# Standing half of the input projection between the steps of self-attention in a fused encoder layer

## The reference

```python
h = rmsnorm(x, norm_mix_g)
proj = h @ w_in
q, k, v, z_sg, gate_logits = jnp.split(proj, IN_SPLITS, axis=-1)
...
attn_branch = block_attention(q, k, v) @ w_attn_o
sg_branch = spatial_gating(jax.nn.gelu(z_sg), sg_norm_g, sg_w, sg_b) @ w_sg_o
g_attn, g_sg = jnp.split(jax.nn.sigmoid(gate_logits), N_BRANCHES, axis=-1)
x = x + (g_attn * attn_branch + g_sg * sg_branch) @ w_out
x = x + cross_attention(rmsnorm(x, norm_xa_g), rmsnorm(mem, norm_mem_g), wq_xa, wkv_xa, wo_xa)
x = x + peer_ffn(rmsnorm(x, norm_ffn_g), w_peer_q, peer_k1, peer_k2, expert_down, expert_up)
```

## Time and profile before

| what | us |
|---|---|
| median of 3 executions | 2597.4 (2597.3 to 2603.41) |
| span of the profiled execution | 2596.5 |
| PE busy in it | 2453.0 (94%) |
| DVE busy | 2168.5 (84%) |
| POOL busy | 1369.1 (53%) |
| ACT busy | 1097.1 (42%) |

### The profile page before, as it was taken

The page is one execution under the profiler, slowest core; times in us unless marked ns, Lnnn a source line. Parts: engine busy times, 40 slices in busy tenths (PEclk is TensorE's granted clock), DMA queues, the critical chain, the costliest instruction groups (busy, mean ns, idle before and its releaser), DMA issues.

```text
span 2596.5 us, 38792 instructions
## 1 busy us (share of the span) xinstructions
PE 2453.0 (94%) x13143; PEld 2072.0 (80%) x13143; DVE 2168.5 (84%) x3950; ACT 1097.1 (42%) x1939; POOL 1369.1 (53%) x1054
## 2 busy tenths in 40 slices
PE   7988999899999999999998889999999999999998
PEld 5767888788876778877876667888888888888987
DVE  6355445886679797877899978999999999999999
ACT  4463444343247313443317993333333333343333
POOL 0000000315742464655665547788788877777875
PEclk9999999999999999999999999999999999999999
DMA  6745545447973788877953559999999999999998
GB/s 249 269 136 178 195 146 178 177 186 270 382 272 114 281 313 320 323 280 259 364 177 135 210 227 402 408 412 415 415 412 415 415 413 415 415 415 400 414 415 310
DMA packets 240423, 787.52 MB, mean 303 GB/s; under 512 B 21904, under 2 KB 75328, under 8 KB 219552
## 3 DMA queue, kind: packets, MB, share of 16 engines
q0 software_dynamic: 112288, 408.77, 40.3%
q1 hardware_dynamic: 128000, 377.00, 39.0%
HBM read 728.01 MB, written 57.67 MB: 303 GB/s over the span
## 4 chain that ended last, share of the span: by engine, by line
PE 33%; DVE 28%; issue 17%; ACT 9%; DMA 8%; POOL 4%; DVEq 1%; POOLq 0%; SPq 0%; ACTq 0%
PE lin L245 9%; PE lin L247 9%; PE lin L246 9%; DVE Y L2454 4%; ACT row_ring L1826 4%; DMA w_raw<-in_up,now 2%; DVE low L2431 2%; DVE w_raw L2440 2%; DVE w_lo L222 2%; DVE low L2420 2%; DVE rows L2440 2%; DVE row_ring L138 2%; PE tr L1755 2%; DMA rows<-in_up,now 2%; DVE gl L2464 1%
## 5 line engine op out<-in xcount | busy, mean ns | idle before, releaser
L150 POOL DMA_INDIRECT row_ring<-in_down,IDX x256 | 365.4, 1428 | 314.2 <-DVE dots L138 241.2
L222 DVE TENSOR_TENSOR w_lo<-w_raw,w_hi 128x2048 fp32r<-128x2048 f32 x100 | 230.1, 2301 | 227.5 <-ACT w_hi L214 213.5
L245 PE MATMUL lin<-w_hi,T_hi 128*128 128x512 f32 x976 | 389.2, 399 | 15.6 <-DVE w_lo L222 7.2
L247 PE MATMUL lin<-w_hi,T_lo 128*128 128x512 f32 x976 | 388.4, 398 | 0.0
L246 PE MATMUL lin<-w_lo,T_hi 128*128 128x512 f32 x976 | 385.9, 395 | 0.0
L214 ACT ACTIVATE w_hi<-w_raw 128x2048 fp32r<-128x2048 f32 x116 | 221.8, 1913 | 351.7 <-PE lin L247 334.4
L2313 POOL DMA_INDIRECT rows<-in_up,now x192 | 309.0, 1609 | 64.7 <-issue 53.9
L138 DVE CUSTOM_DVE_ANT_0 row_ring<-row_ring,H 128x1024 f32<-128x1024 f32 x256 | 302.9, 1225 | 33.6 <-DMA row_ring<-in_down,IDX 32.9
L245 PE MATMUL lin<-w_hi,c_hi 128*128 128x512 f32 x768 | 307.1, 400 | 17.5 <-DVE c_lo L2467 17.3
L2313 POOL DMA_INDIRECT w_raw<-in_up,now x189 | 277.6, 1469 | 84.3 <-issue 43.8
L245 PE MATMUL tr<-T_hi,w_hi 128*128 128x384 f32 x896 | 303.6, 339 | 2.2 <-DVE low L2420 2.2
(11 more groups left out here) (305 smaller groups left out, 5255.2 us busy)
## 6 DMA issues: line engine op xcount, KB each, us to landing
w_raw<-in_wall SPq DMA_DIRECT2D x116, 1024.0 KB
row_ring<-in_up SPq DMA_DIRECT2D x128, 512.0 KB
G<-in_downT SPq DMA_DIRECT2D x112, 512.0 KB
wd<-dense_gates SPq DMA_DIRECT2D x32, 768.0 KB
weight_rests<-w_lo SPq DMA_DIRECT2D x16, 1024.0 KB, 4.9
w_lo<-weight_rests SPq DMA_DIRECT2D x16, 1024.0 KB
dense_gates<-peer SPq DMA_DIRECT2D x6, 2048.0 KB, 6.7
dense_gates<-w_raw SPq DMA_DIRECT2D x5, 2048.0 KB, 6.9
```

The costliest lines, as they stand in the source:

```text
L150: pool.indirect_dma_start(self.ring[:, r % self.K, :], None, self.table, bass.IndirectOffsetOnAxis(ap=self.IDX[:, r:r + 1], axis=0)).then_ ...
L222: dve.tensor_tensor(self.lo[:, h % 2], self.raw[:, h % 2], self.hi[:, h % 2].bitcast(F32), ALU.subtract).then_inc(self.lo_done, 1)
L245: pe.matmul(out, lhs[0], rhs[0], start=start, stop=False, skip_group_check=True)
L247: return pe.matmul(out, lhs[1], rhs[0], start=False, stop=stop, skip_group_check=True)
```

## The change

- The chunks are renumbered so that the spatial gate's v comes before u. `mixer_inputs` now makes 5 chunks (k and v, q, q, v, v) in place of 11.
- A new `attention_and_gates` takes the place of `self_attention`. It has the same steps of attention and puts the other 6 chunks between them: 96 portions in the prompt and 192 in the sample, 6 to a step. In a step PE makes the scores of step s, one transpose group of step s - 1, 1 portion, the other transpose group, 2 portions, the values, 3 portions.
- Scores have one pair of PSUM banks (4 and 5) in place of two, transposes and values one bank each; the probabilities have two buffers in place of three. `keep_busy` between the steps is gone.
- A finished block of attention's output waits in `qT` (whose query is used up) until the projection has read the last of T. Only then is it split into T_hi and T_lo.
- u is stored without Gelu, and `mixer_outputs` applies Gelu to it. The gates are stored as tanh of half their logit, and DVE makes (tanh + 1) times the output, with the factor 0.5 in the turn. Exp and Tanh lie in one table of ACT.
- In `mixer_outputs` the norm moves ahead of the first gated chunk on ACT and DVE, the 6.3 us of `keep_busy` in the sample are gone, and the projection waits block by block (`Heads.upto`).
- Rows in DVE's queue: 50 in `mixer_inputs` and 27 in `self_attention` become 66 in the new stage. The other stages keep theirs, and `bg.finish` takes 23 in place of 12. `choice.soften` and `choice.finish` move into steps 0 and 1 of the new stage.

```diff
-            for c in range(11):
-                st.load(sp, H + 2 * c + 4, min(H + 2 * c + 5, H + 2 * W_AO + 2))
-                spill(c)
...
+        def portions(s):
...
+            return (1, 2, 3) if s < N - 1 else (1, 1, 1) if s == N - 1 else (1, 2, 0)
...
+            split_step = {2 * (c + 1) + half: step_of(at_tile(c, half, NT - 1)) for c in CHUNKS for half in range(2)}
...
             def scores(p):
-                if p >= 2:
-                    pe.wait_ge(exped, 2 * p - 2)
+                if p >= 1:
+                    pe.wait_ge(exped, exped_0 + 2 * p)
...
+            for s in range(N + 1):
+                if s >= 1:
+                    copy(s - 1)
+                if s < N:
+                    exp(s)
...
+                for h, at in split_step.items():
+                    if at == s:
+                        split(h)
...
+            for s in range(N + 1):
...
+                low = [h for h, at in split_step.items() if at == s - 1]
+                for h in low:
+                    st.split_lo(dve, H + h)
+                if not low and s > 1:
+                    bg.dve(dve, 1)
+                if s < N:
+                    norm(s)
...
+                elif s > 1:
+                    bg.dve(dve, 1 if low else 2)
...
-            keep_busy(pe, lin[:, 5], ident, 0.0 if q.first else 6.3)
...
             spills_done(act)
+            norm.act(act)
...
                     bg.dve(dve, 4 if (j, c) == (2, 1) else 8)
+                    if j == 0 and c == 0:
+                        dve.wait_ge(small_in, 48)
+                        norm.dve(dve, Y, sgn[:])
                     st.split_lo(dve, h + 2)
```

More of the change, by code:

```diff
@@ L618, in mixer_inputs @@
         part, roped, turned, copied = (mm.sem(x) for x in ("rope_part", "roped", "qk_turned", "qk_copied"))
-        spilled = [mm.sem(f"spilled{i}") for i in range(STG)]
-        NQ = 3 * NT
-        NALL = 11 * NT
-        spills = [n for n in range(NQ, NALL) if not 5 * NT <= n < 7 * NT]
+        NQ = W_VS * NT
+        NALL = W_U * NT
         SETS = 4 // NT
@@ L673, in between @@
                     qk_turn((c - 1) * NT + i)
-            project_tokens(pe, st, H, 11, T, range(NT), lin, o, between, turn, SETS)
+            project_tokens(pe, st, H, W_U, T, range(NT), lin, o, between, turn, SETS)
         @block.scalar
@@ L697, in copy @@
                 act.activation(dst, src, ACT.Copy).then_inc(copied, 1)
-            for c in range(11):
+            for c in range(W_U):
                 if 1 <= c <= 3:
@@ L703, in _ @@
                 st.split_hi(act, H + 2 * c + 2)
-                if c == SOFTEN and not q.first:
-                    choice.soften(act)
                 for t in range(NT):
@@ L803, in aside @@
                         choice.shift(dve)
-                    if (c, half) == (SOFTEN, 1):
-                        choice.finish(dve)
-                    if (SOFTEN, 0) < (c, half) < (10, 1):
-                        bg.dve(dve, 5)
-            for c in range(11):
+            for c in range(W_U):
                 aside(c, 0)
@@ L884, in attention @@
         bank_units = [last_unit[p["head"]] + 1 for p in banks]
+        (out_hi, out_hi_0), (out_lo, out_lo_0) = (m.carried(f"att_{x}", len(banks)) for x in ("out_hi", "out_lo"))
         @block.tensor
@@ L1012, in _, with gates @@
         @block.tensor
         def _(pe):
+            def gates():
+                for c in CHUNKS:
+                    for half in range(2):
+                        h = H + 2 * c + half
+                        st.wait(pe, h)
+                        for t in range(NT):
+                            bank = NT * (c % SETS) + t
+                            if half == 0:
+                                last = c - SETS
+                                if last < W_U:
+                                    pe.wait_ge(o_first.freed, NT * last + t + 1)
+                                else:
+                                    pe.wait_ge(o.freed, NT * (last - W_U) + t + 1)
+                            for k in range(HK):
+                                kk = half * HK + k
+                                cols = slice(t * P, (t + 1) * P)
+                                x = three(pe, lin[:, bank, :], (T[0][:, kk, cols], T[1][:, kk, cols]),
+                                          (st.hi[:, h % 2, k, :], st.lo[:, h % 2, k, :]),
+                                          start=(kk == 0), stop=(kk == KB - 1))
+                                if k == HK - 1 and half == 1:
+                                    x.then_inc(o.ready, 1)
+                                elif k == HK - 1 and t == NT - 1:
+                                    x.then_inc(st.used, 1)
+                                yield
@@ L1095, in _ @@
+            for n in range(HK, BLOCKS):
+                block_hi(n)
         @block.vector
@@ L1133, in mixer_outputs, with spills_done @@
+            eng.wait_ge(o.freed, UNITS)
+        def spills_done(eng):
+            for i in range(STG):
+                eng.wait_ge(spilled[i], before[i] + 16 * len(range(i, UNITS, STG)))
+        return attended, spills_done, Heads(out_lo, out_lo_0, o.freed, UNITS - NT)
+def mixer_outputs(nc, block, st, q, bg, x_in, T, Y, G, lin, tr, A, U, GA, GS, ident, cleared, attended, spills_done, heads):
     NT, H = q.nt, q.h0 + 2 * W_AO
@@ L1232, in _ @@
                     if j == 0 and c == 0:
-                        norm.act(act)
+                        act.wait_ge(ug_in, 16 * NT)
+                        for t in range(NT):
+                            act.activation(ug[:, t, :], ug[:, t, :], ACT.Gelu_apprx_tanh).then_inc(ug_done, 1)
         @block.vector
```

338 lines of the change are left out of this document (201 added, 137 removed).

## The result

| | before | after |
|---|---|---|
| median, us | 2599.5 (2597.3 to 2603.41, 4 runs) | 2645.32 (2642.97 to 2647.48, 4 runs) |
| span of the profiled execution | 2596.5 | 2645.7 |
| mean granted clock in it | 0.991 | 0.979 |

The ratio is 1.0176, with a 95% interval of 1.0159 to 1.0192. The forecast was 2601 and its range ended at 2617; none of the four cases gives 2645. This ratio, and every ratio further down, is to the kernel before, timed beside the run in question; the kernel before had medians of 2599 to 2602 in these timings.

What follows compares the result with a forecast made beforehand. PE's matmuls bind the first stage, waits in a chain slow attention, and DVE decides in mixer_outputs. Prompt +8.5, sample -22 and rows +17 on 2596.5 gave 2600, or 2601 with 0.9 for the median; range 2584 to 2617.

Steps and rivals of the forecast that it cites:

- four cases: Whole kernel: the forecast 2601 us (chance 0.40) and three rivals, 2589 (0.34), 2619 (0.16) and 2616 (0.10).
- What bounds the kernel: PE's matmuls bind the first stage, DVE a stretch of mixer_outputs; PE delayed at routing's scores delays the end.
- Sample, attention: Sample's attention with chunks between its steps: 253.7 us become 235.4, a gain of 18.3.
- 4.18 + 3.13 = 7.3: Sample's attention: one step is 4.18 us of portions plus 3.13 of PE's attention work, if nothing waits.
- Sample, mixer_outputs: Sample's mixer_outputs: the norm, 5.7 us on DVE, moves into DVE's idle time of 10.65; a gain of 5.
- Prompt, attention: Prompt's attention: waits for split weights, 11.4 us in all, make it +1.2; a slow clock adds +4.2.
- The charge for the clock: Prompt's attention: 1.4 us of slow matmuls after each of three long waits, +4.2.
- Prompt, mixer_outputs: Prompt's mixer_outputs: ACT does the norm before its first split, behind the wait for the last spills; +3 us.
- Rows: Routing's end: 11 more rows left, row 251 comes late, ACT's copy holds PE's scores; +17 us.
- Rival 2: Prompt's attention: PE's short stops make the clock swing in each of 16 steps, costing 22 us; 2619, chance 0.16.
- Rival 1: Small losses in prompt and rows, the sample's gain stays: 2589 us, faster; chance 0.34.
- Rival 3: Sample's attention: late rows make DVE the bound and shrink the gain by 15 us; 2616, chance 0.10.

Runs made afterwards that it cites:

- n2: Changed kernel with the sample's six portions per step at 2, 2, 2 in place of 1, 2, 3, so two stand between the transposes: 2636.39 us.
- n5: Changed kernel with the sample's six portions per step at 2, 4, 0, none after the values: 2630.38 us.
- n10: Changed kernel with early loads for the norm, 11 rows back in attention, the prompt's split ahead of the maximum, sample portions 2, 4, 0: 2583.24 us.
- n6: Changed kernel with the norm still ahead, but its gain and bias loaded by POOL when attention starts, into own buffers: 2633.15 us.
- n3: Changed kernel with the 11 rows put back into the sample's attention, leaving 12 at the end: 2631.91 us.
- n1: Changed kernel with mixer_outputs' norm back in its old place behind the first chunk's second split: 2637.6 us.
- n12: Kernel before the change, without its first 11 rows in the sample's attention, so 23 are left to the end: 2619.02 us.
- n4: Changed kernel with DVE's split of a new half ahead of the step's maximum, in the prompt only: 2635.34 us.
- n11: n10 with the prompt's six portions per step at 1, 5, 0 in place of 1, 2, 3: 2587.85 us.

## Why the prediction was wrong, point by point

- **What bounds the kernel**: right for the places named. PE is the bound in the first stage and DVE in the sample's mixer_outputs, and what delayed PE at the scores delayed the dense matmuls. ("Without a gap" leaves out the 0.69 of the earlier trace rows, too little to matter.)
- **Sample, attention (-18.3; measured -3.4)**: the failed step is "4.18 + 3.13 = 7.3". Both numbers are right, but each was taken from a run of matmuls of one kind. Mixed, a step costs 7.82; n2 gives back 0.30 of it and n5 another 0.19. The cover for ACT's copy and the seams stood in the sum at nothing. I had asked whether DVE keeps up in 7.3 us (it does: n10's steps take 7.29 with 77 rows) and not whether PE itself does. The sign I named for a longer step, PE waiting for w_lo or the norm, didn't appear at all.
- **Sample, mixer_outputs (-5; measured +0.6)**: the failed step is "moves ahead into DVE's idle time". I checked which engines the norm waits for and missed the loads in POOL's queue. n6 shows the size to be right: -4.8.
- **Prompt, attention (+1.2 and +4.2; measured +10.2)**: the waits for split weights are as worked out (10.7 for 11.4). The charge for the clock is near by luck: two slow stretches in place of three, and each dearer than 1.4, cost 3.7 for 4.2; in n3 and n5 three of them cost 6.4 to 6.5. Missing are the seams: a step without a wait takes 6.32 (from 168.41 to 174.73) where I had 6.00, 5.1 us in 16 steps. At the end of the stage 3.8 us pass for the 2.9 of the sum: a wait of 1.54 for a copy at 205.88, and 2.25 from 208.21, behind the last values, to 210.46. These four differences make the 4.8 between 10.2 and the forecast 5.4.
- **Prompt, mixer_outputs (+3; measured +12.6)**: the same late loads, with the slow clock behind the long wait, are 7.7 by n1. The 3 us that I charged to ACT's norm were for the wrong thing: what remains in n1, where the norm is back, is 4.9. By the trace it comes from weights that SP asks for behind the last spills (PE's wait of 2.85) and a clock of 0.87; how it divides is not shown. I had looked at ACT's queue there and neither at POOL's nor at SP's.
- **Rows (+17; measured +19.0)**: right that row 251 holds ACT and ACT holds PE, by the traces, by n3 and, on its own, by n12. PE's idle time was 17.3 for 17; the scores at half speed behind it are 1.5 that stood only in the upper bound. That the size came so near is partly luck, because the way to it was wrong. I took POOL's pitch eleven times and then one row's time. The trace has one stop of 7.38 for row 241, used up 13.2 us after it was asked for, beyond my 11, and then eleven rows at 1.22, near DVE's own pace, which I had kept for the lower bound. The Trainium skill's page "DMA: Bandwidth & Descriptors", section "Anatomy of one DMA — SWDGE (gpsimd) path", gives an estimated 3.2 us for a row. The prediction's "the trace does not agree" was a misreading: its 6.7 us hold the request and the dot product too. For row 240, which took the same 6.65 us, POOL's instruction is 1.76 of them and the dot product 1.21; at most 3.7 are left for the transfer, so this row does not speak against the page.
- **Rival 2 (the clock oscillates)** did not come. In every step PE cycles through single banks, and the sample's stage is at 1.00 throughout; in the prompt only the pieces after long waits are below it, and n4, which all but removes these waits, is at 1.00 over the whole stage. The Trainium skill ("TensorE: Matmul & The Clock Gate", section "A second HAM failure mode: psum-queue depth-cycling") describes a clock that swings because PE pauses often between groups of matmuls while it cycles through PSUM banks; that is not seen here. What the single bank did cost is a wait, 0.30 a step by n2.
- **Rival 1** took the prompt's losses as small; they were 23 us. **Rival 3** is excluded by n3 and n10.
- **What no term covers**: turn to first scores (+5.7) and the last stage (+4.0). Their code is the same. Over the twelve profiles of this study the first of these stretches takes 332.5 to 344.9 us, the second 1257.7 to 1269.7, and neither goes with an edit: n4 has the longest of both, though it touches only the prompt's attention. Much of it is PE's clock. In the first stretch PE is busy for 319.2 us before and 322.1 after with the same 1675 matmuls, at a clock of 0.99 and 0.98 (n4: 327.3 at 0.97; n11: 319.2 at 0.99), and idle for 13.3 and 16.1. In the second it is busy for 5.3 us more and idle for 1.4 less. It stays open why the clock falls more in one execution than in another, and whether part of these 9.7 us belongs to the change. They are also why the medians of single edits differ by some us from what their stretches say.

The range failed because its upper end was built from rivals for the waits that I had thought of, while both passes' terms of the sum lacked costs that go in one direction: seams, the cover for a copy, and late loads.

## What to carry to other kernels

When a step is moved ahead, list every semaphore it waits for, and for a load find the instruction that issues it and what stands ahead of that in its queue: a small load cost ten microseconds here. Matmuls put between those of another kind hid a wait here only where they lasted as long as the copy and both handovers of the single bank (n2), and each change of kind had a price of about 0.1 us (n5). So few large pieces are better than many small ones, as long as no place loses its cover by it (n11). Background work taken out of one stage doesn't vanish: look for the wait at its end before taking any out.

## What was not expected of the hardware

- The start after a projection's matmul is 0.23 us later if another such matmul or a transpose follows, and 0.32 to 0.33 if values or scores follow; after a projection's first matmul behind transposes or values it is 0.31 to 0.33 too. All of it is counted as busy time. Removing two of five such places per step gave 0.19 us (n5).
- Of three equal waits of 2.65 us in the prompt, the clock fell after the last two in the kernel after, n1 and n2, and not after the first (1.00 over the 10 us around it). In n3, n5 and n6, with the same waits, it fell after the first too (0.66, 0.66 and 0.83).
- The distance from the request for a row to the end of its dot product was 6.65 us for row 240, 13.2 for row 241 and 8.8 for row 251. From row 241 on the rows landed some 1.22 us apart while the DMA engines were 0.99 busy, though POOL had asked for them 1.66 apart.
